# Where twelve pieces of dense work stand among the small products of a hybrid decoder's rounds

## The reference

```python
h = _rmsnorm(x, p['norm_mix_pre'])
z = h @ p['w_in']
za = z[..., :SHIFT_W]                         # RWKV-7 branch
zb = z[..., SHIFT_W:SHIFT_W + RET_W]          # retention branch: q, k, v, gate
...
ya, s_wkv, s_shift = _rwkv7_branch(za, ...)   # S = S*w - (S kk) b^T + v k^T ; y = S r, token by token
yb, s_ret = _retention_branch(zb, ...)
m = sigmoid(ga) * (ya @ w_out_a) + sigmoid(gb) * (yb @ w_out_b)
x = x + _rmsnorm(m @ w_o, norm_mix_post)
f = (silu(h2 @ w_ffn_gate) * (h2 @ w_ffn_up)) @ w_ffn_down
x = x + _rmsnorm(f, norm_ffn_post)
```

## Time and profile before

| what | value |
|---|---|
| median of 3 runs | 1270.49 us (1269.52 to 1271.22) |
| span of the profiled execution | 1270.8 us |
| PE matmuls busy | 1221.7 us, 96% of the span, 12056 instructions |
| PE weight loads busy | 1157.7 us, 91% |
| DVE busy | 855.3 us, 67% |
| ACT busy | 558.2 us, 44% |
| POOL busy | 152.7 us, 12% |
| rounds, layer 0 and layer 1 | 53.00 us and 51.72 us |
| weight transfers w_raw<-wts | 282 of 512 KB, 3.5 us from issue to landing |

### The profile page before, as it was taken

The page is one execution under the profiler, slowest core; times in us unless marked ns, Lnnn a source line. Parts: engine busy times, 40 slices in busy tenths (PEclk is TensorE's granted clock), DMA queues, the critical chain, the costliest instruction groups (busy, mean ns, idle before and its releaser), DMA issues.

```text
span 1270.8 us, 27906 instructions
## 1 busy us (share of the span) xinstructions
PE 1221.7 (96%) x12056; PEld 1157.7 (91%) x12056; DVE 855.3 (67%) x1468; ACT 558.2 (44%) x849; POOL 152.7 (12%) x168
## 2 busy tenths in 40 slices
PE   6999899999999999999989998999999999999996
PEld 5999788998998999999978987889999989999996
DVE  4887558878776666663378864687878576666433
ACT  4553345455536333343355544444563453333432
POOL 0004456100000000000000062840100000000000
PEclk9999899999999999999999999999999999999999
DMA  6433144644453644444424432364444535444441
GB/s 215 143 116 122 40 118 146 250 127 144 123 166 102 221 150 150 150 149 150 150 91 126 134 100 74 103 212 172 148 159 135 163 107 166 152 143 154 153 149 67
DMA packets 51466, 179.13 MB, mean 141 GB/s; under 512 B 6288, under 2 KB 7568, under 8 KB 50064
## 3 DMA queue, kind: packets, MB, share of 16 engines
q1 hardware_dynamic: 42576, 153.77, 38.5%
q10 hardware_dynamic: 8768, 23.58, 5.2%
HBM read 166.18 MB, written 8.53 MB: 137 GB/s over the span
## 4 chain that ended last, share of the span: by engine, by line
PE 83%; DVE 9%; ACT 4%; issue 2%; DMA 1%; ACTq 0%; SPq 0%; DVEq 0%
PE dense L1388 52%; PE core L1388 31%; DVE w_lo L912 2%; ACT w_hi L599 1%; DVE x L962 1%; DVE y_out L960 1%; DMA ret_s<-ret_t 1%; DMA x<-x_t 0%; ACT L587 0%; DVE ret_t L1257 0%; DVE bonus L1031 0%; DVE tmp L1017 0%; ACT sq_pair L822 0%; ACT h_hi L605 0%; DVE bonus L1027 0%
## 5 line engine op out<-in xcount | busy, mean ns | idle before, releaser
L912 DVE TENSOR_TENSOR w_lo<-w_raw,w_hi 128x1024 fp32r<-128x1024 f32 x282 | 352.7, 1253 | 220.1 <-ACT w_hi L599 219.5
L599 ACT ACTIVATE w_hi<-w_raw 128x1024 fp32r<-128x1024 f32 x282 | 297.6, 1057 | 415.5 <-PE dense L1388 273.3
L1388 PE MATMUL dense<-h_hi,w_hi 128*128 128x320 f32 x1296 | 415.3, 320 | 20.1 <-DVE w_lo L912 11.3
L1388 PE MATMUL dense<-h_lo,w_hi 128*128 128x320 f32 x1296 | 403.0, 311 | 0.0
L1388 PE MATMUL dense<-h_hi,w_lo 128*128 128x320 f32 x1296 | 402.8, 311 | 0.0
L1388 PEld LDWEIGHTS dense<-h_hi,w_hi 128*128 128x128 f32 x1296 | 245.5, 189 | 40.2 <-issue 30.8
L1388 PEld LDWEIGHTS dense<-h_lo,w_hi 128*128 128x128 f32 x1296 | 245.9, 190 | 1.3 <-issue 0.2
L1388 PEld LDWEIGHTS dense<-h_hi,w_lo 128*128 128x128 f32 x1296 | 245.7, 190 | 0.0
L1388 PE MATMUL core<-h_hi,w_hi 128*128 128x320 f32 x416 | 129.3, 311 | 0.4 <-DVE w_lo L912 0.4
L1388 PE MATMUL core<-h_hi,w_lo 128*128 128x320 f32 x416 | 128.7, 309 | 0.0
L1388 PE MATMUL core<-h_lo,w_hi 128*128 128x320 f32 x416 | 128.7, 309 | 0.0
(11 more groups left out here) (306 smaller groups left out, 1994.1 us busy)
## 6 DMA issues: line engine op xcount, KB each, us to landing
w_raw<-wts SPq DMA_DIRECT2D x282, 512.0 KB, 3.5
ret_t<-ret_t ACTq DMA_DIRECT2D x16, 256.0 KB, 3.4
ret_s<-ret_t ACTq DMA_DIRECT2D x16, 256.0 KB, 2.4
ret_rest<-ret_d ACTq DMA_DIRECT2D x2, 1536.0 KB, 8.2
qk_rot<-qk_raw SPq DMA_DIRECT2D x8, 320.0 KB, 6.4
dmask<-rconst ACTq DMA_DIRECT2D x2, 1152.0 KB, 5.4
s_st<-wkv_st ACTq DMA_DIRECT2D x2, 1024.0 KB, 4.9
wkv_s<-s_st ACTq DMA_DIRECT2D x2, 1024.0 KB, 4.3
```

The lines of the kernel that those rows point to most:

```text
L599: act.activation(w_hi[n % RING][:, :], w_raw[n % RING][:, :], ACT.Copy).then_inc(hi_ready.sem, 1)
L912: dve.tensor_tensor(w_lo[r][:, :], w_raw[r][:, :], w_hi[r][:, :].bitcast(F32), ALU.subtract).then_inc(low_made.sem, 1)
L1388: return pe.matmul(out, lhsT, rhs, start=start, stop=stop)
```

## The change

The slots behind which the twelve pieces stand are other ones. Nothing else is altered: the same 48 slots, the same matmuls, the same splits at the slots of `LOW_AT` (10, 18, 30 and 42).

```diff
 THIRDS = ((0, 3), (3, 6), (6, 8))
-PIECE_AT = {at: (n // 3, THIRDS[n % 3]) for n, at in enumerate((2, 5, 8, 12, 16, 20, 24, 28, 32, 37, 42, 48))}
+PIECE_AT = {at: (n // 3, THIRDS[n % 3]) for n, at in enumerate((2, 5, 9, 13, 17, 21, 25, 29, 33, 37, 41, 45))}
 LOW_AT = {10: 1, 18: 2, 30: 3, 42: 4}
```

## The result

The changed kernel takes 1272.62 us as median of 20 runs (1268.49 to 1279.71), the kernel before on the same chip 1268.88 us (20 runs, 1266.26 to 1276.23): ratio 1.0027, 95% interval 1.0016 to 1.0039. So it costs some 3.5 us. The forecast was 1269.8 us against 1270.49, no measurable difference; the time lies in its range, the direction does not.

A forecast was written before the change was run, and what follows sets the result against it. TensorE's rounds were taken as bound by code fetches in blocks of 256 instructions. Layer 0 -2.35 and layer 1 +1.65 us, both less 0.1, gave -0.9 us; forecast set at 1269.8 us, range 1266.2 to 1274.6.

The forecast's parts named there:

- (b), the clock: Layer 0's rounds: with the gap in slot 37 shrunk, no half clock follows and the next block gains 2.1 us.
- (b), layer 0, the starving block: Block of slots 34 to 37: a weight transfer moves ahead of its code fetch, 3.76 instead of 4.65 us, -0.9 us.
- (b), layer 1: Earlier weight transfers against code fetches: first met, 1.4 us, second missed, third met, 1.8 us; +3.2 us.
- missed by 0.25 us: Layer 1, behind slot 17: transfer at 3.65 us, code fetch at 3.4 us, so no meeting and no cost.
- (c), layer 1, the blocks of 4.14 and 4.18 us: Layer 1's rounds: two blocks lengthened by a running weight transfer fall to 3.76 us, -0.8 us.
- wrong at the root: Sign against the whole forecast: block stretches well under 3.7 us in either layer.
- (a): Slot 8's piece moved behind slot 9: m_sq wait gone, block limit at slot 22's end about 0.5 us earlier.
- (c): Last piece, slot 48 to 45: hidden in layer 1, -1.1 us; wait ahead of w' +1.15 and +0.75 us.
- C: Rival, slower: layer 1's slot 20 fetch also caught, +2.0 us, and a clock drop, 2.1 us; 1273.7 us, chance 0.2.
- D: Rival, no change: layer 0's gap still lowers the clock, or a fetch there is caught; 1271.7 us, 0.2 with E.
- The page's rule: Code fetch across blocks is mostly hidden, so only engine waits count: about 1 to 1.5 us slower.
- bound between 1.36 and 1.67 us: Gap length above which the clock drops; layer 0's gap of about 1.4 us was taken as no drop.

The follow-up runs named there:

- e4: The kernel before, unchanged, profiled a second time: 1270.24 us, ratio 0.9998.
- f3: The kernel before, unchanged, one more profiled execution: rounds 49.71 and 51.02 us, rest of the span 1166.9 us.
- f2: The changed kernel once more, on another chip: ratio 1.0032 to the kernel before; rounds 50.61 and 54.14 us.
- f4: The changed kernel, one more profiled execution: rounds 51.79 and 54.41 us, rest of the span 1170.3 us.
- e5b: The kernel before with the four weight loads during each layer's rounds cut to 16 of 1024 columns: 1269.79 us, ratio 1.0001.
- e7: The changed kernel with ScalarE's copy of value tile 3 back at slot 48: 0.52 us of wait left ahead of w' in layer 0.
- e6b: The changed kernel with the four weight loads during each layer's rounds cut to 16 of 1024 columns: 1267.62 us, ratio 0.9988.
- e9b: The kernel before with 64 already met waits, 32 instructions, added at TensorE's start: 1272.53 us.
- e11: The changed kernel with 160 already met waits, 80 instructions, added at TensorE's start: 1269.53 us, ratio 1.0000.
- f1: The kernel before with 160 already met waits, 80 instructions, added at TensorE's start: 1271.61 us, ratio 1.0021.
- e3: The kernel before with only the seven pieces of slots 8 to 32 moved one slot later: 1273.92 us, ratio 1.0023.
- e1: The changed kernel with the last piece and ACT's values(3) put back behind slot 48: 1272.47 us, ratio 1.0014.

## Why the prediction was wrong, step by step

- **The base.** The forecast sets the span of 1270.8 us beside the median of 1270.49 as if the two were the same measure. The span leaves out some 1.8 us of an execution's time (1268.7 and 1270.47 us for the changed kernel), so the profiled execution of the kernel before took about 1272.6 us (an estimate), 2.1 above the median. Layer 0's 53.00 us were part of that: e4 and f3 have 50.85 and 49.71.
- **(b), the clock, -2.1 us: the step that failed.** It took the half clock of rows 8 as what this kernel always pays. Two of three executions don't, and two of three of the changed kernel have 3.4 us of half clock in their rounds. A gain of 2.1 us was booked against a cost that is mostly not there and that the change does not remove. Layer 0 was to gain 2.45 us; in the means it is 0.3 us longer (51.4 against 51.2).
- **(b), layer 0, the starving block, -0.9 us: nearly right.** From crossing to crossing it takes 4.65, 4.11 and 3.55 us in the three executions before and 3.50, 3.52 and 3.27 us in the three changed: -0.7 in the mean. A cost behind it was not seen: e_sq of slot 34 now stands on ACT behind `values` of slot 33, and PE stands idle for 0.78 us ahead of its use in slot 36 (f2, f4), inside the time of the fetch. The record calls this issue, but in f2 e_sq ends 0.1 us before PE goes on.
- **(b), layer 0, a term left out.** Three transfers were checked against fetches in layer 1 but not in layer 0. The fetch of slot 19's limit is caught there in every execution: gap in slot 22 of 1.75, 1.48, 1.75 us against 0.5, which is +1.1 us and takes the gain back.
- **(b), layer 1.** The meetings at slot 12 and slot 31 came as forecast (1.9 to 2.3 and 2.9 to 3.1 us from crossing to packet, the second with the gap of 2.01 us). That of slot 20 was "missed by 0.25 us" on paper and was met in all three, with gaps of 1.21, 0.98 and 1.48 us in slot 23 against 0.39, 0.80 and 0.39 before, +0.7 in the mean. A margin of a quarter microsecond, worked out from sums of rounded slot times, decides nothing. Layer 1 as a whole: +1.55 forecast with two meetings, +2.2 measured.
- **(c), layer 1, the blocks of 4.14 and 4.18 us, -0.8 us: half of it.** The forecast read both as lengthened by a transfer. The second takes 3.73 us in f2 and f4. The first takes 4.15, 4.16 and 4.14 us in the changed kernel and 4.14 us in e5b, where no large transfer runs. Nor is 3.76 us the least time of a block, as the sign "wrong at the root" has it: the starving block took 3.27 us in f4.
- **(a) right.** The m_sq wait is gone. Counted from the first product of layer 0's rounds, the crossing in slot 19 comes at 20.5, 20.9 and 20.5 us before and at 20.0, 20.1 and 20.1 us changed, some 0.6 us earlier, where 0.5 was forecast for slot 22.
- **(c) right, slightly off in size:** the wait ahead of w' is 0.86 us in layer 0 (1.15 forecast) and 0.86, 0.52, 0.52 us in layer 1 (0.75), and the last piece is hidden in layer 1. In layer 0 ACT was named rightly (e7).
- **The rivals.** C, slot 20's fetch caught and one long gap that lowers the clock, 1273.7 us, has the right events in layer 1: the meeting in all three executions, half clock at 774.23 us behind the gap of 2.01 in one of them. Its figure is close to 1272.62 by luck. It gives the meeting 2.0 us, where the gap grew by 0.7, a clock drop to every execution, and keeps layer 0's gain of 2.35 us, which did not come. D's second half, a fetch of layer 0 that is caught, came too. C had a chance of 0.2, for a margin too small to carry that.
- **The page's rule.** "Mostly hidden" in the Trainium skill's "Runtime: NRT & Kernel Launch", section "Instruction fetch mechanics", gave +1 to 1.5 us by waits for engines alone. The time rose by more than that, and for another reason: with those waits and no transfers e6b has a ratio of 0.9988, at most 1.0007, which leaves the waits at most 0.9 us (against e5b it is lower too, with a wider scatter).

## What to carry to other kernels

Where TensorE runs many short instructions, its code is one more load on the DMA engines: list the limits of its blocks and the starts of the large transfers on one time line before you move work, and check every transfer in every repetition of the stage. Take no term below 3 us from one profile of a kernel whose executions differ by as much; read the same stretch in a second execution first. And an experiment that shifts the code but not the work (e9b, e11, f1) separates "what the order costs" from "where its code happens to lie".

## What the runs showed of the hardware

- PE's code comes in packets of 0.02 MB, one for 256 instructions: 95 of them in the kernel before, 96 with 80 instructions more (e11). In the later part of the rounds, with no large transfer (e5b, e6b), the packet starts 1.1 to 1.7 us behind the crossing, most often 1.2. If a 512 KB transfer starts first, the packet starts when that is about through, up to 3.4 us behind the crossing (e3). PE's stall comes at the next limit, up to 2.7 us long (e1).
- A block of 2.3 us of work takes 3.8 to 4.1 us from crossing to crossing even with no large transfer at all (e5b, e6b), and 3.3 to 3.6 at best (f4, f3).
- The clock's answer to a gap is not fixed by its length. Half clock followed gaps of 2.28 us, 2.01 us (changed, layer 1), 1.75 us (f4, slot 22), 1.87 us (e9b) and 1.73 us (e1, slot 37; e3, slot 22), but not the same 2.01 us in f2 and f4, 1.73 us in e4 and e6b, or 2.68 us in e1. The forecast's bound between 1.36 and 1.67 us had no ground.
- 64 waits in a row on TensorE became 32 instructions and 160 became 80. They cost nothing ahead of the first weights (first matmul at 9.87 us with and without the 80): a free way to move all later block limits.
